# Last layer of a three-layer block: equal scores chosen by replacing first places, and a search opened with fewer steps

## The reference

```
rel   = einsum('bqhd,bsd->bqhs', iqb, ik)                  # 8 small heads of 64
score = einsum('bqh,bqhs->bqs', iwb, relu(rel))            # one score for each key
score = where(key_pos <= t, score, -inf)
_, sel = top_k(score, 256)                                 # the 256 best keys of each query
logits = q . kv_sel * R_KV ** -0.5 + bias(dist)            # over those keys alone
o      = softmax(logits) @ kv_sel
```

## Time and profile before

| | us |
|---|---|
| median of 3 runs (4018.71 to 4019.96) | 4018.75 |
| the profiled execution | 4022.36 |
| its span | 4020.2 |
| the stage with the change, from its first logits read at 2831.4 | 1188.8 |

### The profile page before, as it was taken

How to read it: one execution, slowest core, us unless ns; L and a number is a source line. 1 busy time by engine, 2 the same in 40 slices (tenths; PEclk the granted TensorE clock), 3 DMA queues, 4 the chain that set the end, 5 groups by cost and what they waited for, 6 DMA issues and landing times. The chain is left out here.

```text
span 4020.2 us, 59813 instructions
## 1 busy us (share of the span) xinstructions
PE 3828.9 (95%) x23330; PEld 2665.3 (66%) x23330; DVE 2639.0 (66%) x4954; ACT 1358.7 (34%) x2905; POOL 922.8 (23%) x542
## 2 busy tenths in 40 slices
PE   8999999998999999998999999998999999998887
PEld 5565555555566666665888888886665656665544
DVE  5565666655777777764566666564366777788885
ACT  1222222222111111112333333332354545665562
POOL 0444344434222333331222222222000000000000
PEclk9999999999999999999999999998999999999998
DMA  7333343343544443425000000003210000000000
GB/s 257 141 137 142 126 153 121 116 147 110 195 141 154 154 146 136 138 102 169 25 22 25 28 23 28 22 10 103 76 36 24 32 24 19 32 19 19 19 3 29
DMA packets 199263, 342.12 MB, mean 85 GB/s; under 512 B 22277, under 2 KB 102474, under 8 KB 198858
## 3 DMA queue, kind: packets, MB, share of 16 engines
q1 hardware_dynamic: 198986, 338.26, 23.9%
HBM read 298.90 MB, written 39.33 MB: 84 GB/s over the span
## 5 line engine op out<-in xcount | busy, mean ns | idle before, releaser
L271 PE MATMUL e_ps<-arena 128*128 128x386 f32 (+1 forms) x1960 | 653.8, 487 | 5.8 <-DVE arena L321 2.9
L271 PEld LDWEIGHTS e_ps<-arena 128*128 128x128 f32 x1960 | 364.6, 191 | 250.5 <-issue 19.3
L271 PE MATMUL o_ps<-arena 128*128 128x320 f32 x1624 | 462.3, 436 | 16.3 <-PEq L67 3.8
L1757 PE MATMUL d_ps<-hT_in,arena 128*128 128x128 f32 x3072 | 393.5, 283 | 6.6 <-ACT hT_in L1982 4.6
L271 PEld LDWEIGHTS o_ps<-arena 128*128 128x128 f32 x1624 | 301.4, 191 | 145.7 <-issue 16.9
L1757 PEld LDWEIGHTS d_ps<-hT_in,arena 128*128 128x128 f32 x3072 | 360.6, 193 | 22.2 <-ACT hT_in L1982 5.8
L2726 PE MATMUL s_ps<-s_w_out,arena 128*128 128x512 f32 x512 | 242.9, 612 | 0.0
L2523 PE MATMUL s_ps<-hT_in,arena 128*128 128x128 f32 x2016 | 234.2, 275 | 0.0
L2523 PEld LDWEIGHTS s_ps<-hT_in,arena 128*128 128x128 f32 x2016 | 230.4, 192 | 2.4 <-issue 1.4
L663 PE MATMUL e_ps<-e_w_out,e_gt 128*128 128x512 f32 x512 | 223.7, 595 | 0.0
L1204 PE MATMUL o_ps<-o_w_out,o_gt 128*128 128x512 f32 x512 | 223.4, 594 | 0.0
(11 more groups left out here) (541 smaller groups left out, 6927.1 us busy)
## 6 DMA issues: line engine op xcount, KB each, us to landing
arena<-l_w_in SPq DMA_DIRECT2D x48, 1024.0 KB, 7.7
arena<-l_w_in SPq DMA_DIRECT2D x32, 1040.0 KB, 8.3
xb<-x SPq DMA_DIRECT2D x64, 512.0 KB, 4.3
arena<-l_w_in SPq DMA_DIRECT2D x16, 1544.0 KB, 8.9
arena<-l_w_in SPq DMA_DIRECT2D x16, 1280.0 KB, 7.6
arena<-l_w_in SPq DMA_DIRECT2D x32, 504.0 KB, 6.8
arena<-l_w_in SPq DMA_DIRECT2D x16, 768.0 KB, 7.3
o_scratch<-w_ada SPq DMA_DIRECT2D x16, 768.0 KB
```

The source lines that it names most:

```text
L271: m = pe.matmul(bank[(g + k) % 2][:, 0:self.n], rows[:, kk * P:(kk + 1) * P], cols[:, kk, :], start=(kk == 0 and k in (0, 1, 4)), stop=(kk ...
L1757: m = pe.matmul(bank[c % 2][:, t * P:(t + 1) * P], W_in[:, k, (4 * c + t) * P:(4 * c + t + 1) * P], hT[:, k * P:(k + 1) * P], start=(k == ...
```

## The change

1. `equal_scores` works otherwise. `choose` keeps its 8 best (`best`) and the number of missing places (`cnt`) instead of overwriting them. In the branch those of the 8 that lie beyond the missing place are made unmatchable (3e38 is added), `match_replace` replaces the first occurrence of each of the others in `work` by -3e38, and where a score equal to `thr` is left, `selb` is lowered.
2. The bounds are taken earlier where W > 1024: `lo` and the largest of the first 1024 (or W-255) scores (`ahead`) in the second half of the iteration before, ahead of the 19th and of the 21st weighing. `start_search` takes what is left.
3. The first middle is made from `hi` and `lo`; `nsteps` and `steps` are made behind the first count.
4. POOL does the gate of block i+1 ahead of the addition of row block i.
5. The `mix_rows` of block 13 is moved in iteration 14 from behind `set_aside` to behind `choose`. ACT waits for it before it makes the next row's mean.

```diff
             def equal_scores(W):
-                step_(dve.tensor_scalar(work[:, 0:W], acc[:, 0:W], thr[:, 0:1], 0.0, ALU.is_equal, ALU.add, accum_out=equals[:]), 1)
-                step_(dve.tensor_tensor(cnt[:], equals[:], cnt[:], ALU.subtract), 2)
-                step_(dve.tensor_scalar(cnt[:], cnt[:], 1.0, float(TOPK), ALU.mult, ALU.add), 3)
-                step_(dve.tensor_tensor_scan(other[:, 0:W], work[:, 0:W], work[:, 0:W], 0.0, ALU.add, ALU.max), 4)
-                step_(dve.scalar_tensor_tensor(work[:, 0:W], other[:, 0:W], cnt[:, 0:1], work[:, 0:W], ALU.is_gt, ALU.mult), 5)
-                step_(dve.scalar_tensor_tensor(selb[:, 0:W], work[:, 0:W], -FAR, selb[:, 0:W], ALU.mult, ALU.add), 6)
+                step_(dve.tensor_scalar(match[:], iota[:], cnt[:, 0:1], 3e38, ALU.is_gt, ALU.mult), 1)
+                step_(dve.tensor_tensor(best[:], best[:], match[:], ALU.add), 2)
+                step_(dve.match_replace(other[:, 0:W], best[:], work[:, 0:W], -3e38), 3)
+                step_(dve.tensor_scalar(other[:, 0:W], other[:, 0:W], thr[:, 0:1], -FAR, ALU.is_equal, ALU.mult), 4)
+                step_(dve.tensor_tensor(selb[:, 0:W], other[:, 0:W], selb[:, 0:W], ALU.add), 5)
             def start_search(j):
-                dve.tensor_reduce(lo[:], acc[:, 0:TOPK], AX.X, ALU.min).then_inc(*o.inc())
-                do(dve.tensor_reduce(hi[:], acc[:, 0:W - TOPK + 1], AX.X, ALU.max))
-                do(dve.tensor_scalar(hi[:], hi[:], lo[:, 0:1], None, ALU.subtract))
+                bounded = W - TOPK + 1
+                if W <= 2 * WIDE:
+                    (the three lines above, unchanged)
+                elif bounded <= 2 * WIDE:
+                    do(dve.tensor_scalar(hi[:], ahead[:], lo[:, 0:1], None, ALU.subtract))
+                else:
+                    do(dve.tensor_reduce(hi[:], acc[:, 2 * WIDE:bounded], AX.X, ALU.max))
+                    do(dve.tensor_scalar(hi[:], hi[:], ahead[:, 0:1], lo[:, 0:1], ALU.max, ALU.subtract))
                 dve.memset(few[:], W - 2 * TOPK + 1.5).then_inc(*o.inc())
-                dve.tensor_scalar(nsteps[:], halves[:], hi[:, 0:1], -1.0, ALU.mult, ALU.mult).then_inc(*o.inc())
-                do(dve.tensor_scalar(steps[:], halves[:], hi[:, 0:1], None, ALU.mult))
-                do(dve.tensor_scalar(mid[:], steps[:, 0:1], lo[:, 0:1], None, ALU.add))
+                do(dve.tensor_scalar(mid[:], hi[:], 0.5, lo[:, 0:1], ALU.mult, ALU.add))
             def search(j, turn):
-                    do(dve.tensor_scalar(passed[:, 0:W], ..., accum_out=cnt[:]))
+                    dve.tensor_scalar(passed[:, 0:W], ..., accum_out=cnt[:]).then_inc(*o.inc())
+                    if n == 0:
+                        (nsteps and steps, as above)
+                    o.settle()
             def choose(j):
                 (best is kept and kth takes its place; the last count goes to equals, not cnt)
             iteration i:
-                if i == HELD + 1:
-                    mix_rows(i - 1, own.hT, 0)
                 dve.wait_ge(*exp_ready.upto(i))
...
                 if searched:
                     choose(j)
+                    if i == HELD + 1:
+                        mix_rows(i - 1, own.hT, 0)
                     dve.wait_ge(*pv_made.upto(i))
                     check_chosen(j)
                 def weigh(numbers):
                     for n in numbers:
+                        if n == 18:
+                            dve.wait_ge(*relu_used.upto(i + 2, 16))
+                            dve.tensor_reduce(lo[:], acc[:, 0:TOPK], AX.X, ALU.min).then_inc(*o.inc())
+                        if n == 20:
+                            bounded = min(2 * WIDE, (i + 3) * P - TOPK + 1)
+                            dve.tensor_reduce(ahead[:], acc[:, 0:bounded], AX.X, ALU.max).then_inc(*o.inc())
                         dve.wait_ge(*relu_ready.upto(i + 2, n + 1))
         POOL:
+            gate(0)
             for i in range(BLOCKS):
-                if i != HELD + 1:
-                    gate(i)
                 ckv_rows(i + 2)
-                if i == HELD:
-                    gate(i + 1)
                 if i == BLOCKS - 1:
                     break
+                gate(i + 1)
                 pool.wait_ge(*mix_ready.upto(i))
                 (the row addition)
         ACT, in root_rows(i), behind the wait for the squares:
+                if i == HELD + 1:
+                    act.wait_ge(*mix_ready.upto(HELD))
```

More of the change, by code:

```diff
@@ L2621, in sparse_layer @@
         hi = sb("hi", [P, 1])
+        ahead = sb("ahead", [P, 1])
         mid = sb("mid", [P, 1])
@@ L2634, in sparse_layer @@
         thr = sb("thr", [P, 1])
+        kth = sb("kth", [P, 8])
         bad = sb("bad", [P, 2])
@@ L3027, in start_search @@
                 W = (j + 1) * P
-                dve.tensor_reduce(lo[:], acc[:, 0:TOPK], AX.X, ALU.min).then_inc(*o.inc())
-                do(dve.tensor_reduce(hi[:], acc[:, 0:W - TOPK + 1], AX.X, ALU.max))
-                do(dve.tensor_scalar(hi[:], hi[:], lo[:, 0:1], None, ALU.subtract))
+                bounded = W - TOPK + 1
+                if W <= 2 * WIDE:
+                    dve.tensor_reduce(lo[:], acc[:, 0:TOPK], AX.X, ALU.min).then_inc(*o.inc())
+                    do(dve.tensor_reduce(hi[:], acc[:, 0:bounded], AX.X, ALU.max))
+                    do(dve.tensor_scalar(hi[:], hi[:], lo[:, 0:1], None, ALU.subtract))
+                elif bounded <= 2 * WIDE:
[3 more added lines that the diff above has]
+                    do(dve.tensor_scalar(hi[:], hi[:], ahead[:, 0:1], lo[:, 0:1], ALU.max, ALU.subtract))
                 dve.memset(few[:], W - 2 * TOPK + 1.5).then_inc(*o.inc())
-                dve.tensor_scalar(nsteps[:], halves[:], hi[:, 0:1], -1.0, ALU.mult, ALU.mult).then_inc(*o.inc())
-                do(dve.tensor_scalar(steps[:], halves[:], hi[:, 0:1], None, ALU.mult))
-                do(dve.tensor_scalar(mid[:], steps[:, 0:1], lo[:, 0:1], None, ALU.add))
+                do(dve.tensor_scalar(mid[:], hi[:], 0.5, lo[:, 0:1], ALU.mult, ALU.add))
             def search(j, turn):
@@ L3044, in search @@
                 for n in range(first, first + SHARES[turn][0]):
-                    do(dve.tensor_scalar(passed[:, 0:W], acc[:, 0:W], mid[:, 0:1], 0.0, ALU.is_ge, ALU.add, accum_out=cnt[:]))
+                    dve.tensor_scalar(passed[:, 0:W], acc[:, 0:W], mid[:, 0:1], 0.0, ALU.is_ge, ALU.add, accum_out=cnt[:]).then_inc(*o.inc())
+                    if n == 0:
+                        dve.tensor_scalar(nsteps[:], halves[:], hi[:, 0:1], -1.0, ALU.mult, ALU.mult).then_inc(*o.inc())
+                        dve.tensor_scalar(steps[:], halves[:], hi[:, 0:1], None, ALU.mult).then_inc(*o.inc())
+                    o.settle()
                     do(dve.tensor_scalar(step[:], cnt[:], TOPK - 0.5, steps[:, n:n + 1], ALU.is_ge, ALU.mult))
@@ L3067, in choose @@
                 dve.tensor_scalar(match[:], iota[:], cnt[:, 0:1], 0.0, ALU.is_equal, ALU.add, accum_out=step[:]).then_inc(*o.inc())
-                do(dve.scalar_tensor_tensor(best[:], iota[:], cnt[:, 0:1], best[:], ALU.is_equal, ALU.mult, accum_out=thr[:]))
-                dve.tensor_scalar(passed[:, 0:W], acc[:, 0:W], thr[:, 0:1], 0.0, ALU.is_ge, ALU.add, accum_out=cnt[:])\
+                do(dve.scalar_tensor_tensor(kth[:], iota[:], cnt[:, 0:1], best[:], ALU.is_equal, ALU.mult, accum_out=thr[:]))
+                dve.tensor_scalar(passed[:, 0:W], acc[:, 0:W], thr[:, 0:1], 0.0, ALU.is_ge, ALU.add, accum_out=equals[:])\
                    .then_inc(*chosen.inc())
@@ L3072, in choose @@
                 o.settle()
-                dve.tensor_scalar(bad[:, 1:2], cnt[:], step[:, 0:1], TOPK - 0.5, ALU.mult, ALU.is_lt).then_inc(*o.inc())
-                dve.tensor_scalar(bad[:, 0:1], cnt[:], float(TOPK), None, ALU.not_equal).then_inc(*bad_ready.inc())
+                dve.tensor_scalar(bad[:, 1:2], equals[:], step[:, 0:1], TOPK - 0.5, ALU.mult, ALU.is_lt).then_inc(*o.inc())
+                dve.tensor_scalar(bad[:, 0:1], equals[:], float(TOPK), None, ALU.not_equal).then_inc(*bad_ready.inc())
             def check_chosen(j):
```

## The result

| | before | after |
|---|---|---|
| median (4 runs each) | 4018.73 | 3990.22 |
| profiled execution | 4022.36 | 3986.74 |
| start of the changed stage | 2831.4 | 2824.0 |
| stage, first logits read to the last instruction | 1184.8 | 1156.6 |

A forecast was written before the change was run, and what follows sets the result against it. PE was taken to bound the kernel, DVE's savings counting only where PE waits. Branch 16.1, held mix 1.35 and opening 5.8, less bounds 4.9 and gate 2, gave 16.3 us: 4018.75 to 4002.4, range 3991 to 4011.

The forecast's parts named there:

- What bounds the kernel: PE is busy 95% of the span, DVE 66%; time saved on DVE counts only where PE waits for it.
- Step 1: Equal-scores branch on DVE: 6.4 instead of 11.9 us at W = 2048; 16.1 us gained in iterations 5, 6, 11, 12, 14.
- Step 3: Search opening from mix_rows to first count: head 1's idle on PE in iterations 5 to 11 goes, 5.8 us gained.
- Step 4: Early bounds on DVE ahead of weighings 19 and 21: 4.9 us lost over iterations 8, 9, 10, 12, 13, 14.
- Step 5: POOL's gate first: DVE additions L3114 and L3117 wait for it in some of iterations 6 to 13, 2 us lost.
- Step 2: Held mix moved behind choose in iteration 14: PE's transposes, early matmuls and L2853 come earlier, 1.35 us gained.
- Sum: All terms together: 16.1 + 1.35 + 5.8 - 4.9 - 2 = 16.3 us faster, giving 4002.4.
- C: Late iterations follow DVE: opening gives 2.6 more in 12 and 13 each, gate meets nothing; 3990 to 3995; chance 0.15.
- A: match_replace is slow: 4009 at two cycles per column, chance 0.10; slower than now beyond 3.4 cycles, chance 0.03.
- B: Second half pays for the opening: early bounds cost 12.5 us, gate 8; time 4016; chance 0.08.
- D: The branch's time isn't PE's: something late refills the idle, leaving half, 8 us; time 4010.5; chance 0.06.

The follow-up runs named there:

- 4, undone: The whole change but with POOL's old order (gate behind the row addition): ratio 0.9923 to the kernel before, stage 1154.5 against 1156.6 of the whole change.
- part 1 alone: The kernel before with only equal_scores by replacement and its bookkeeping: 3999.3, ratio 0.9948, stage 20.5 us less.
- parts 1, 3 and 5: The whole change with bounds and POOL's order as before: ratio 0.9916, stage 1150.8; once more 3988.79, ratio 0.9919, stage 1153.3.

## Why the prediction was right or wrong

- **What bounds the kernel**: right. PE's idle places were the right ones; that they were the whole of it was wrong, for the clock and for the hidden part of the waits.
- **Step 1, equal scores, 16.1**: the branch itself is right to 0.1 us (6.4 foreseen, 6.5 measured) and so is the price of the instruction that no row showed. The step that failed is its last one, that the end gains what DVE saves behind an idle time and no more. The part alone gives 20.5. What I left out is in the earlier trace rows only as idle time: around it the clock is at 1.2 GHz. Iteration 6 gave 4.4 for 2.8 of DVE's time, with its only 3.4 us of low clock gone; 11 gave 5.7 for 4.5, 12 and 13 5.8 for 4.9 (the sum's own 5.5 at 2048 columns gives 4.8 at 1792, and DVE saved 4.8), 5 0.75 for 0.3; 14 with the start of 15 gave 3.8 for 3.6. The clock's share fits in 6 and 11; in 5 there was no low clock, and how the excess divides elsewhere stays open.
- **Step 3, opening, 5.8**: the step that failed most, by what it counted as PE's waits. That POOL sets the 3.98 us was right, that 12 to 14 gain nothing too. But I let only head 1's idle in 5 to 11 go. It is 11.7, 2.2 of it in iterations 1 to 4, which I had at nothing. ACT works through head 1 in order, so with the search its copies came earlier too, and PE's waits for these shrank by 2.5; in narrow iterations head 3's exponential counted; and the shift at head 1's transposes was in each iteration from 3 to 11 by 0.16 or 0.17 longer than the idle time that the trace shows there. Why is open.
- **Step 4, early bounds, -4.9**: right in sign, too dear in size. Alone the stage grew by 2.4, undone it fell by 0.5. Without the low clock that moved in iteration 15 it is 3.7 and 3.6, without 11's as well 2.3 and 2.0. The 1.5 at the end of 13 came out as 1.0.
- **Step 5, gate, -2**: right (2.1 when undone), beside part 3; alone the move gains, which the step didn't say. Additions of two SBUF tensors waited for the gate: 0.28 became 1.33 and 1.01 in iterations 6 and 7, 0.43 became 1.36 and 1.51 in 10 and 15. By the Trainium skill, page "SBUF — State Buffer", section "SBUF: two separate sides", a VectorE operation with two SBUF inputs and a GpSimd one that reads SBUF exclude each other for a whole instruction; these numbers agree.
- **Step 2, held mix, 1.35**: 1.31 where I said. Alone, 0.67 of it came back by the clock.
- **Sum**: by whole stages 20.5 (part 1), 11.1 (3) and 1.1 (5), less 2.4 (2), all alone, less 2.1 (4, undone), is 28.2, and the stage gave 28.2. That it fits so closely is in part luck, as stretches of low clock moved by 1.3 to 1.7 in most runs. And it holds only with part 4's price beside the others: alone it gained 6.8, and with that the sum would be 37.1.
- **Rivals**: C had the right time (3990 to 3995) for a wrong reason: 12 and 13's first halves gained 0.2 and 0.1, not 2.6. A fell by the replacement's 2.27, B by second halves that paid 3.7 at most where it had 12.5, D by the 20.5 of part 1. The range failed for the same reason as the forecast: I bounded the opening by 5.8 above and the branch by DVE's saving, from idle time shown, with nothing for the clock and for waits not shown. Its lower end of 3991 came from rival C, for reasons that did not hold, so that it was missed by only 0.8 us is luck.

## What to carry to other kernels

An idle time of PE can cost more than its length: look at the granted clock around it, and price the part of the low clock in which PE works with it. When an engine in the middle of a chain gets its input earlier, count everything that it does in order behind it, not only the first wait that it ends. And try the parts of a change one by one: here two of five only cost beside the others. One of these, the gate's move, gained when it stood alone, but part 3 had already bought the same.

## What was not expected of the hardware

Parts of a stage that an edit doesn't touch repeated within 0.05 us from trace to trace over some 1150 us, while whole runs of one kernel spread by 4 to 12 us. What differs is the layers ahead (the stage began at 2824.0 to 2831.7 us) and where stretches of low clock of 3.4 us fall: the changed kernel's two traces differ in one such stretch, in iteration 10 behind 2.3 us of idle PE, and in nothing else over 0.05 us. Nor does the same idle time always bring the low clock: ahead of the score matmuls of iteration 11 PE is idle for 2.44 us with part 1 alone and with parts 1, 3 and 5; no low clock follows in the first, 3.4 us of it in the second, and that half is 1.3 us longer there.
